# Running sums of the stick-breaking mixer: one PSUM bank per head, extended block by block, issued between the next head's scores

## The reference

```python
def stickbreaking_mixer(qkv):
    q, k, v = [t.reshape(B_, S_, SB_HEADS, HEAD_DIM) for t in jnp.split(qkv, 3, axis=-1)]
    scale = HEAD_DIM ** -0.5
    for c in range(S_ // Q_BLOCK):
        z = jnp.einsum('bqhd,bkhd->bhqk', q[:, t0:n_k], k[:, :n_k]) * scale
        mask = jnp.arange(n_k)[None, :] < t[:, None]
        log_nb = jnp.where(mask, -jax.nn.softplus(z), 0.0)
        after = lax.cumsum(log_nb, axis=3, reverse=True) - log_nb
        weights = jnp.where(mask, jnp.exp(jax.nn.log_sigmoid(z) + after), 0.0)
        outs.append(jnp.einsum('bhqk,bkhd->bqhd', weights, v[:, :n_k]))
```

## Time and profile before

| what | value |
|---|---|
| median of three runs | 2307.31 us |
| the profiled execution, its own time | 2303.84 us |
| its span | 2302.1 us |
| mean granted TensorE clock | 0.959 of full speed |
| PE busy | 2120.3 us (92%) |
| DVE busy | 1144.4 us (50%) |
| ACT busy | 758.9 us (33%) |
| POOL busy | 538.6 us (23%) |

### The profile page before, as it was taken

How to read it: one execution, slowest core, us unless ns; L and a number is a source line. 1 busy time by engine, 2 the same in 40 slices (tenths; PEclk the granted TensorE clock), 3 DMA queues, 4 the chain that set the end, 5 groups by cost and what they waited for, 6 DMA issues and landing times.

```text
span 2302.1 us, 25818 instructions
## 1 busy us (share of the span) xinstructions
PE 2120.3 (92%) x10100; PEld 1676.2 (73%) x10100; DVE 1144.4 (50%) x1575; ACT 758.9 (33%) x1149; POOL 538.6 (23%) x300
## 2 busy tenths in 40 slices
PE   5989998899999899999988889888999998999998
PEld 3667976667677688888756679766566776888886
DVE  6344569763347544432273365796533475444321
ACT  5333231264334322222152332313642343222221
POOL 2336027523116000000032350374131250000000
PEclk9999999999989999999989999999989899999999
DMA  4232011222124223333233310123121342332332
GB/s 144 101 104 80 15 46 60 83 69 69 55 102 166 80 92 100 94 100 101 67 99 101 117 49 15 51 69 97 55 69 42 126 153 69 100 101 92 101 101 92
DMA packets 55124, 197.03 MB, mean 86 GB/s; under 512 B 6112, under 2 KB 6112, under 8 KB 52576
## 3 DMA queue, kind: packets, MB, share of 16 engines
q1 hardware_dynamic: 43488, 161.85, 22.1%
q10 hardware_dynamic: 11520, 33.56, 3.8%
HBM read 176.51 MB, written 18.87 MB: 85 GB/s over the span
## 4 chain that ended last, share of the span: by engine, by line
PE 36%; DVE 8%; POOL 2%; ACT 2%; DMA 1%; issue 1%; SPq 0%; POOLq 0%; DVEq 0%; PEldq 0%; ACTq 0%
PE bank L455 9%; PE bank L457 9%; PE bank L456 9%; DVE arena L1636 2%; DVE arena L1631 1%; DMA raw<-weights 1%; PE bank L904 1%; PE bank L662 1%; PE bank L865 1%; PE bank L642 1%; POOL wL L1859 1%; PE bank L792 1%; DVE wL L1320 1%; DVE arena L1802 1%; ACT wH L1005 0%
## 5 line engine op out<-in xcount | busy, mean ns | idle before, releaser
L455 PE MATMUL bank<-hH,wH 128*128 128x512 f32 (+1 forms) x1536 | 620.7, 404 | 54.9 <-POOL wL L1859 27.4
L456 PE MATMUL bank<-hL,wH 128*128 128x512 f32 (+1 forms) x1536 | 609.9, 397 | 0.0
L457 PE MATMUL bank<-hH,wL 128*128 128x512 f32 (+1 forms) x1536 | 608.4, 396 | 0.0
L1859 POOL TENSOR_TENSOR wL<-raw,wH 128x1024 fp32r<-128x1024 f32 x114 | 281.6, 2474 | 1232.7 <-ACT wH L1005 1232.5
L1005 ACT ACTIVATE wH<-raw 128x1024 fp32r<-128x1024 f32 x276 | 290.2, 1053 | 395.9 <-PE bank L457 231.7
L455 PEld LDWEIGHTS bank<-hH,wH 128*128 128x128 f32 (+1 forms) x1536 | 294.9, 192 | 135.3 <-issue 36.4
L457 PEld LDWEIGHTS bank<-hH,wL 128*128 128x128 f32 (+1 forms) x1536 | 293.6, 191 | 65.6 <-issue 1.0
L456 PEld LDWEIGHTS bank<-hL,wH 128*128 128x128 f32 (+1 forms) x1536 | 294.4, 192 | 61.8 <-issue 1.0
L1320 DVE TENSOR_TENSOR wL<-raw,wH 128x1024 fp32r<-128x1024 f32 x162 | 213.3, 1317 | 185.3 <-ACT wH L1005 185.2
L1008 ACT ACTIVATE gst<-bank 128x512 f32<-128x512 f32 x64 | 38.2, 596 | 351.1 <-PE bank L457 351.1
L457 PE MATMUL bank<-hidH,wL 128*128 128x512 f32 x352 | 140.4, 399 | 0.0
(11 more groups left out here) (380 smaller groups left out, 3008.1 us busy)
## 6 DMA issues: line engine op xcount, KB each, us to landing
raw<-weights SPq DMA_DIRECT2D x296, 512.0 KB, 3.5
gates<-gst ACTq DMA_DIRECT2D x64, 256.0 KB, 2.4
gload<-gates ACTq DMA_DIRECT2D x16, 1024.0 KB, 6.9
xT<-x SPq DMA_DIRECT2D x1, 2048.0 KB, 10.1
out<-xT SPq DMA_DIRECT2D x1, 2048.0 KB, 6.7
const<-constants SPq DMA_DIRECT2D x1, 1228.5 KB, 5.5
pack<-params SPq DMA_DIRECT2D x2, 451.0 KB, 3.9
cosT<-pos SPq DMA_DIRECT2D x1, 256.0 KB, 5.6
```

The costliest lines, as they stand in the source:

```text
L455: mm(out, a[0], b[0], start=start, stop=False)
L456: mm(out, a[0], b[1], start=False, stop=False)
L457: return mm(out, a[1], b[0], start=False, stop=stop)
L1859: tt_(wL[:, ORD[i] % SPLIT], raw[:, i % RING], wH[:, ORD[i] % SPLIT].bitcast(F32), SU)\
```

## The change

Three edits, all in the stick-breaking part.

1. The sums of a head stay in one bank, 4 + h % 2, at the columns of their queries. For key block 3 the bank gets the triangle "ge" of that block, as before. For each further block kb two matmuls are added to what the bank holds: "lt" on block kb + 1 (which completes that block's triangle to a full matrix of ones, 128*(3 - kb) columns) and "ge" on block kb (128*(4 - kb) columns). 7 matmuls a head.
2. Since "lt" goes on in the bank that DVE reads, it waits until `sb_weight` of the item before is done (`d_ready` >= n); before, item n waited for item n - 2 (`d_ready` >= n - 1).
3. PE issues scores and sums in alternation, one item each; DVE issues abs of the new head, weight and mask of the old one in alternation.

```diff
-                        if n >= 2:
-                            pe.wait_ge(q["d_ready"], n - 1)
-                        out = PS[4 + n % 2]
-                        for j in range(kb, NT):
-                            last = mm(out[:, P * (j - kb):S - P * kb], cst("ge") if j == kb else ones,
-                                      sb_sp(h, j)[:, P * j:S], start=(j == kb), stop=(j == NT - 1), skip_group_check=True)
-                        last.then_inc(q["cum_ps"], 1)
+                        out = PS[4 + h % 2]
+                        if kb < 3:
+                            pe.wait_ge(q["d_ready"], n)
+                            mm(out[:, P * kb + P:S], cst("lt"), sb_sp(h, kb + 1)[:, P * kb + P:S],
+                               start=False, stop=False, skip_group_check=True)
+                        elif h >= 2:
+                            pe.wait_ge(q["d_ready"], n - 4)
+                        mm(out[:, P * kb:S], cst("ge"), sb_sp(h, kb)[:, P * kb:S],
+                           start=(kb == 3), stop=True, skip_group_check=True).then_inc(q["cum_ps"], 1)
...
                     for h in range(H + 1):
-                        if h < H:
-                            for j in range(4):
-                                sb_scores(4 * h + j)
                         if h == 1:
                             pe.wait_ge(q["s5_done"], 2)
-                        if h:
-                            for j in range(4):
+                        for j in range(4):
+                            if h < H:
+                                sb_scores(4 * h + j)
+                            if h:
                                 sb_sums(4 * h - 4 + j)
                         fill(FILL["sb"][h])
...
-                        stt(z, PS[4 + n % 2][:, 0:S - P * kb], -1.0, z, M, A_).then_inc(q["d_ready"], 1)
+                        stt(z, PS[4 + h % 2][:, P * kb:S], -1.0, z, M, A_).then_inc(q["d_ready"], 1)
...
                     for h in range(H + 1):
-                        if h < H:
-                            for n in range(4 * h, 4 * h + 4):
+                        for n in range(4 * h, 4 * h + 4):
+                            if h < H:
                                 sb_abs(n)
-                        if h:
-                            for n in range(4 * h - 4, 4 * h):
-                                sb_weight(n)
-                                sb_weight_mask(n)
+                            if h:
+                                sb_weight(n - 4)
+                                sb_weight_mask(n - 4)
```

## The result

The changed kernel takes 2326.01 us (median of 10 runs, 2318.64 to 2339.46) against 2307.33 us (median of 10, 2302.64 to 2311.08): a ratio of 1.0091 [1.0068, 1.0114], 18.7 us or 0.9% slower. Forecast was 2325. In a later group of runs it stands at 2326.84 against 2304.88 (1.0079 [1.0052, 1.0107]).

The account below looks back on a forecast made before the run. PE was taken as the bound, busy for 2120.3 of 2302.1 us. Turns 1 to 4 and the clock, 2.5 + 0.3 + 0.5 + 3.0 + 2.5 = 8.8 us a layer, 17.6 for both, gave 2325; range 2309 to 2338.

Parts of the forecast that it names:

- Four pieces fewer, only if PE is waited for: PE's sums: 16 pieces of 128 columns a head, not 20, saving 0.86 us a head, 6.9 in all.
- The chain of 5.2 us from the first weight: PE and DVE handovers: a turn's sums end 5.2 us after its first weight, at full clock.
- Turn 1, +2.5: Values of turn 1 start at 487.6 against 485.11, behind slower sums and ACT's later exps: +2.5 us, bounds 0 and +2.5.
- The slow case: Turn 1 with PE at 1.2 GHz up to 481.80: sums end at 483.8, values start at 487.6, +2.5 us.
- Turns 2 and 3, first weights at 3.4 and 3.2 us: DVE's first weight ends that far into the turn, so sums end at 8.6 and 8.4 us: +0.3 and +0.5.
- Turn 4, +3.0: Sums of turn 4, without scores to hide the chain: taken as +3.0 us, between +2.3 and +4.1 by POOL's split.
- The forecast case: Turn 4: the first weight passes during POOL's split, its mask is held, the second weight comes at 2.8 us: +2.3.
- The clock, +2.5 (bounds 0, 7.5): Emptier turns 2 to 4 drop PE to 1.2 GHz: one hit of 2.5 us a layer, bounds 0 and 7.5.
- Rival C: The clock drops in every turn, PE at 1.2 GHz through most of the sums: 2335 us; chance 0.12.
- POOL against DVE: POOL's split locks out DVE's abs and masks with two SBUF inputs until it ends; used in turns 3 and 4.
- What would show it: Signs in the profile after, such as 14 instructions a head, PE waiting before most "lt", turn 4's sums 7 us or more.
- rival A: Scores hide handovers, first weights come early, clock stays full: -3.8 us a layer, 2300; decides at 2.4 us; chance 0.13.

Follow-up runs that it names:

- splits_late: The changed kernel with POOL's splits at turns 1, 3 and 4 held until DVE has done the turn's masks: 2311.96 us.
- tile_begun: The changed kernel with one filler in each of five turns, 6 of its 24 matmuls ahead of the first "lt" in turns 1 to 4: 2319.70 us.
- interleave_splits_late: The kernel before, ten matmuls in two banks, with the new order on PE and DVE and POOL's splits held until the turn's masks are done: 2298.51 us.

## Why the prediction was right, and where it was not

The sign was right, and each mechanism of the forecast is in the traces: the chain, POOL's lock, ACT late in turn 1, a lower clock. That the sum came out at 2325 for 2326 is luck. The waits were forecast at 6.3 us a layer and the clock at 2.5. The medians leave 0 to 6 us in all for the waits and give the clock 13 us or more: two errors cancel.

**Four pieces fewer, only if PE is waited for.** Right in its place. Without the chain and in before's order the two parts of the profile are 5.9 us shorter, of 6.9. The median wins 2.2 us, within noise.

**The chain of 5.2 us from the first weight.** Right at full clock. With splits late, turn 3 takes 6.79 and 6.91 us, where 6.8 was worked out for it undisturbed. Turn 4 undisturbed takes 5.88, not 6.6, since DVE's softplus was done before the turn began. Against the same order without the chain this is 0.1 to 0.2 us in turn 3 and 1.7 in turn 4. What costs more is that the chain hands on a delay of DVE: without it a first abs held for 1.60 us left turn 3 at 6.68, with it one held for 1.15 us came with a wait of 0.93 before the first "lt" and a fall of the clock.

**Turn 1, +2.5.** The slow case came, but for +1.3 and +1.5. The first abs was not held as in the earlier trace rows: this turn began at 476.21, 4.7 us later than in the earlier trace rows, and the abs at 478.12 took 0.29. It was the mask of the first weight that POOL held (DVE, then POOL; the row of 475.89 is two splits, the second from 478.20 to 480.62):

```profile
478.12 0.29 DVE L1662 SCALAR_TENSOR_TENSOR pj<-arena 128x128 f32<-128x128 f32 x1 [2.41 <-ACT arena L1198]
...
478.65 2.12 DVE L1688 TENSOR_TENSOR arena<-arena,const 128x128 f32<-128x128 f32 x1
```

```profile
475.89 4.73 POOL L1859 TENSOR_TENSOR wL<-raw,wH 128x1024 fp32r<-128x1024 f32 x2 [3.04 <-ACT wH L1006]
517.16 2.35 POOL L1859 TENSOR_TENSOR wL<-raw,wH 128x1024 fp32r<-128x1024 f32 x1 [36.54 <-ACT wH L1006]
```

The next abs and weight of DVE stand behind that mask, and PE's second "lt" waits for them. And the values followed the sums by 1.77 us, not 3.8: with PE at 1.2 GHz ACT's table load and the four exps of the new head were done under the sums, and only the four exps of weights stood behind them.

**Turns 2 and 3, first weights at 3.4 and 3.2 us.** Over-sized: they ended 1.85 and 2.3 us into the turn. ACT was less late than I had it, so DVE's backlog was smaller, and POOL's split ran from 0.5 us before turn 3 to 1.84 us into it, not from 0.3 to 2.7. It held the abs for 1.15 us, as foretold in kind.

**Turn 4, +3.0.** The forecast case came, the weight passing and its mask held (0.27 and 0.95 us at 539.21 and 539.52, as 0.27 and 0.96 in the earlier trace rows), but on a DVE that was less late: +1.3 in layer 1. In layer 2, with the clock low, +3.3.

**The clock, +2.5 (bounds 0, 7.5). This is the step that failed.** I priced a low stretch like the one in the earlier trace rows, 6.5 us long and 2.5 us a hit, and took one of them a layer beside the one that turn 1 had before. That is 13 us more at 1.2 GHz in the program. The medians have 34 to 41 more, the two parts of the profile 58 more (72 against 14), and its layer 1 is longer by 2.2 us in the values of turn 1, 4.3 in turn 2, 3.7 in turn 3 and 3.0 in the fillers behind these turns. What I had missed is how long such a stretch lasts once it is there. I took it to end when PE is busy again, as it did in the earlier trace rows. In layer 1 it ended only in the next filler, in layer 2 after 17.0 us. Rival C (2335) is near what the profiled execution shows, with the clock down in three turns of layer 1; the median lies between it and mine.

**POOL against DVE.** This was the step that mattered most. The terms for turns 3 and 4 rested on it, and splits_late gave 14 of 24 us back. But the forecast had it as a wait of DVE alone. With the splits late the medians have 29 us less at 1.2 GHz, worth 10 to 14 of these 14: the wait empties PE, and the clock follows. Idle matmuls in the waits give 6 us back, late splits 14, both 19 of the 24.

The Trainium skill ("TensorE: Matmul & The Clock Gate", "What's actually happening") states that the array's slow state is the default and activity releases it. The trace agrees on the fall, which in the two parts came each time in a turn with open waits. PE's busy time alone doesn't tell when the clock comes back: in layer 1 PE was busy for 15.10 of 15.10 us at 0.50, in layer 2 it came back 1.3 us into turn 2.

**What would show it.** 14 instructions a head, ACT's L1209 as the releaser of the values of turn 1, and a clock of 0.5 in turns 2 to 4 were all there. PE waited for L1682 before half of the "lt" (12 of 24), not before most. Turn 4's sums of 7 us or more were there in one layer of two. POOL's splits keep the number L1859, since the two files are equally long: only lines between the first edit on PE and the one in DVE's order moved, by one or two. And rival A's bound of 2.4 us for the first weight fits a loss of 3.0 us in turn 4; with the 2.1 of its own sum it is 2.8.

## What to carry to other kernels

Before two items are put in one accumulator to save matmuls, count the handovers that this adds against the matmuls: here three waits a head for 0.86 us of work. Where an engine's wait leaves TensorE's queue short of work, look behind the wait for the granted clock of the next 20 us, and judge by the clocks of several executions, since one profile can be at either end, and much of its low clock can lie where nothing was changed. And look first for an instruction that no one is waiting for and that holds the one all wait for: holding back three splits of POOL a layer made the same new order some 15 us faster (2314.04 to 2298.51).

## What the runs showed of the hardware

- The clock stayed at 1.2 GHz for 30.7 us with PE busy for 28.1 of them. The work there was scores (64 of 128 rows of the array), short sums of 128 to 512 columns and values (64 columns of it). In layer 1 it was back within 2 to 3 us of the filler's 128x128 by 512 matmuls in turns 2 and 3; in layer 2 it came back at 1661.1 under scores and sums, with no filler. In tile_begun six matmuls of a filler ran at 1.2 GHz and the clock didn't come back. What decides it isn't settled here.
- A turn can be fuller, hardly shorter, and cost less: turn 1 up to its values with PE busy for 8.20 of 11.40 us kept the full clock (interleave_splits_late), and with 7.33 of 11.60 it was followed by 20.5 us at 1.2 GHz (splits_late). These are one execution each.
- A lock between POOL and DVE holds a two-input instruction of DVE that comes during the split, for what is left of it: 2.12 us, 1.15 and 0.95 of splits of 2.34 to 2.42, while the weight that reads PSUM passed at 0.28 in turn 1 and 0.27 in turn 4.
